# A decoder step on one core: fewer key steps carried over, unit-matrix products during the first loads, the gates' sums between tile products

## What is computed

```python
mod = silu(c) @ w_ada + b_ada                  # 3072 columns: shift, scale, gate
h = rms_norm(x, norm_g) * (1 + scale) + shift
z = h @ w_in                                   # columns split into
#   att q | k | v | silu-gate (512 each), mLSTM q,k | v | o | silu-gate, i,f gate logits, two merge gates
A = attend(q, k, v)       # 8 heads x 64; samples: top-3 past blocks of 256 keys by q . mean(k), paged cache
B = mlstm(qk, v, i, f)    # 4 heads; gates need cumsum(log sigmoid f) and a running maximum
ya = (A * silu(za)) @ w_att ; ym = (B * silu(zm)) @ w_mlstm
x = x + gate * ((sigmoid(ga) * ya + sigmoid(gm) * ym) @ w_out), then a last RMSNorm
```

## Time and profile before

| | us |
|---|---|
| median of 3 runs (lowest, highest) | 733.54 (732.51, 970.24) |
| the profiled execution, its device time | 734.37 |
| its span in the trace | 731.4 |
| busy in the span: TensorE / DVE / GpSimd / ScalarE | 685.4 / 470.9 / 429.9 / 334.2 |
| bytes moved | 144.72 MB, mean 198 GB/s |

### The profile page before, as it was taken

One profiled execution on the slowest core, in us unless ns is written; L12 is line 12 of the kernel. 1 busy time (PEld: TensorE's weight loads), 2 busy tenths in 40 slices (PEclk: granted clock), 3 DMA queues, 4 the chain that ended last, 5 costly groups with the idle time before them and its releaser, 6 DMA issues.

```text
span 731.4 us, 14741 instructions
## 1 busy us (share of the span) xinstructions
PE 685.4 (94%) x5012; PEld 611.4 (84%) x5012; DVE 470.9 (64%) x483; ACT 334.2 (46%) x726; POOL 429.9 (59%) x278
## 2 busy tenths in 40 slices
PE   1799999998989979999999999999999999999996
PEld 0477788887868858999999999997899998999974
DVE  0625579998979964995697597762445368444435
ACT  5546556656471436464464544514322224322643
POOL 4203366576756417698789688752754656566520
PEclk9997999999998999999999999999899999999999
DMA  8978359888898777387867668758475355832302
GB/s 314 340 232 252 114 159 297 245 269 266 244 268 262 243 211 214 96 242 209 242 199 209 201 199 241 219 163 226 124 199 148 99 176 155 252 96 86 87 28 90
DMA packets 156904, 144.72 MB, mean 198 GB/s; under 512 B 7547, under 2 KB 115152, under 8 KB 156852
## 3 DMA queue, kind: packets, MB, share of 16 engines
q1 hardware_dynamic: 142984, 137.15, 62.5%
q10 hardware_dynamic: 13876, 7.02, 3.2%
HBM read 135.10 MB, written 9.11 MB: 197 GB/s over the span
## 4 chain that ended last, share of the span: by engine, by line
PE 59%; SPq 12%; DVE 10%; issue 7%; POOL 5%; DMA 5%; ACT 1%; ACTq 0%; DVEq 0%; POOLq 0%
PE ps L556 42%; SPq L398 5%; SPq L399 4%; DMA sb_arenaA<-in_w_ada 3%; PE ps L990 3%; PE ps L822 2%; DVE sb_arenaA L1833 2%; POOL sb_arenaA L1563 2%; POOL sb_arenaA L1595 2%; POOL sb_wL L1517 2%; PE ps L930 1%; PE ps L590 1%; DVE sb_arenaA L1980 1%; DVE sb_arenaB L1980 1%; PE ps L783 1%
## 5 line engine op out<-in xcount | busy, mean ns | idle before, releaser
L1517 POOL TENSOR_TENSOR sb_wL<-sb_wraw,sb_wH 128x512 fp32r<-128x512 f32 (+1 forms) x168 | 222.3, 1338 | 202.0 <-ACT sb_wH L1020 183.6
L556 PE MATMUL ps<-sb_hH,sb_wH 128*128 128x260 f32 x1152 | 241.7, 292 | 0.9 <-ACT sb_arenaB L1025 0.9
L556 PE MATMUL ps<-sb_hH,sb_wL 128*128 128x260 f32 x1152 | 235.4, 286 | 0.0
L556 PE MATMUL ps<-sb_hL,sb_wH 128*128 128x260 f32 x1152 | 235.2, 286 | 0.0
L556 PEld LDWEIGHTS ps<-sb_hH,sb_wH 128*128 128x128 f32 x1152 | 181.5, 193 | 15.7 <-issue 13.4
L1020 ACT ACTIVATE sb_wH<-sb_wraw 128x512 fp32r<-128x512 f32 (+1 forms) x168 | 99.3, 612 | 195.8 <-PE ps L556 159.9
L556 PEld LDWEIGHTS ps<-sb_hL,sb_wH 128*128 128x128 f32 x1152 | 181.4, 192 | 0.0
L556 PEld LDWEIGHTS ps<-sb_hH,sb_wL 128*128 128x128 f32 x1152 | 181.0, 192 | 0.0
L1595 POOL TENSOR_TENSOR sb_arenaA<-sb_arenaA 128x2048 f32<-128x2048 f32 x28 | 101.6, 3633 | 1.7 <-DMA sb_arenaA<-in_cache_v 1.7
L1837 DVE TENSOR_REDUCE sb_arenaA<-sb_arenaA 128x2048 f32 (+1 forms) x32 | 72.9, 2284 | 3.8 <-DVE sb_arenaA L1833 2.5
L1563 POOL TENSOR_TENSOR sb_arenaA<-sb_arenaA 128x2048 f32<-128x2048 f32 x11 | 54.4, 4941 | 28.2 <-DMA sb_arenaA<-in_cache_k 28.2
(11 more groups left out here) (389 smaller groups left out, 976.6 us busy)
## 6 DMA issues: line engine op xcount, KB each, us to landing
sb_wraw<-in_w_in SPq DMA_DIRECT2D x64, 512.0 KB, 5.2
sb_arenaA<-in_cache_k SPq DMA_DIRECT2D x128, 256.0 KB, 3.1
sb_arenaA<-in_cache_v SPq DMA_DIRECT2D x128, 256.0 KB, 3.1
sb_arenaA<-in_w_ada SPq DMA_DIRECT2D x6, 2048.0 KB, 12.4
sb_arenaB<-in_state_C SPq DMA_DIRECT2D x8, 512.0 KB, 3.9
sb_wraw<-in_w_mlstm SPq DMA_DIRECT2D x8, 512.0 KB, 5.1
sb_wraw<-in_w_out SPq DMA_DIRECT2D x8, 512.0 KB, 3.8
sb_arenaB<-in_x_prompt SPq DMA_DIRECT2D x1, 2048.0 KB
```

Of the source, the lines that this page charges most:

```text
L556: last = mm(ps[:, 2 * s + a, 0:HALF], w[:, s, k, :], x[:, k, a * HALF:(a + 1) * HALF], start=(k == 0 and w is wH and x is xH), stop=(k == ...
L1517: tt(wL[:, j % 2, part], wraw[:, j % 4, part], wH[:, j % 2, part].bitcast(F32), ALU.subtract)\
```

## The change

- `keep_clock(bank, count)` multiplies the unit matrix with itself, 512 columns, into a bank that is overwritten later: seven products ahead of the first `modulation`, four ahead of the third.
- In the first pair the gates' running sums (now `forget_sums`) stand between the products of the first half of the v tile, and the two turns and the key and value transposes each move behind a further half tile; `ptrans(0)` moves ahead of the value transposes. ScalarE's `normalise(0)` and the high part of tile n + 4 move ahead of the key eviction in the first pair.
- DVE carries steps 6 and 5 into the next pair, no longer 7. In the first pair step 2 is taken ahead of head 1's maximum, and step 3 after head 1's inverse sums. In the loop the products of steps 6 and 0 are parted from their sums.
- After the last pair the fourth mLSTM tile moves ahead of the selection's products, and the sixth is multiplied whole ahead of the last `modulation`; ScalarE's high part of the sixth moves with it.

```diff
@@ -609,7 +609,12 @@
                         last = tr(ps[:, 4 + k % 4, j * P:(j + 1) * P], xt[:, j, k * P:(k + 1) * P], ident[:, :])
                     last.then_inc(t_x, 1)
 
+            def keep_clock(bank, count):
+                for _ in range(count):
+                    mm(ps[:, bank, :], ident[:, :], ident[:, :].unsqueeze(1).broadcast_to([P, TT, P]), start=True, stop=True)
+
             pe.wait_ge(consts, 2)
+            keep_clock(6, 7)
             modulation(0, 0)
             pe.wait_ge(x_nrm, 2)
             prompt_turn(range(4))
@@ -626,6 +631,7 @@
 
             pe.wait_ge(v_col, 1)
             pe.wait_ge(mod_rdy, 2)
+            keep_clock(3, 4)
             modulation(2, 2)
             ztile(0, T_ATT, hH, hL, part_ready=h_lo, parts=(0,))
             pe.wait_ge(xT_dve, 5)
@@ -680,6 +686,15 @@
                     last = mm(ps[DH * e:DH * e + DH, 7, k * P:T], vN[:, k, DH * e:DH * e + DH], pT[:, k, k * P:T],
                               start=(k == 0), stop=(k == TT - 1))
                 return last
+
+            def forget_sums(ks):
+                for j in ks:
+                    pe.wait_ge(g_dve, 3)
+                    last = mm(ps[:, 7, MH * j:MH * j + MH], upper[:, :], lf[:, j, :], start=True, stop=(j == 0))
+                    for i in range(j):
+                        last = mm(ps[:, 7, MH * j:MH * j + MH], ones[:, :], lf[:, i, :], start=False, stop=(i == j - 1))
+                    if j == TT - 1:
+                        last.then_inc(g_pe, 1)
 
             def query_copy(e, t, bank):
 
@@ -715,42 +730,41 @@
                 query_copy(0, t, 4)
                 if before:
                     pv(1).then_inc(pv_done, 1)
-                else:
-                    pe.wait_ge(g_dve, 3)
-                    for j in range(TT):
-                        last = mm(ps[:, 7, MH * j:MH * j + MH], upper[:, :], lf[:, j, :], start=True, stop=(j == 0))
-                        for i in range(j):
-                            last = mm(ps[:, 7, MH * j:MH * j + MH], ones[:, :], lf[:, i, :], start=False,
-                                      stop=(i == j - 1))
-                    last.then_inc(g_pe, 1)
                 pe.wait_ge(z_free, n + 4)
                 qk(0, t)
-                ztile(2, n + 2, hH, hL, parts=(0, 1) if before else (0,))
-                if not before:
-
+                if before:
+                    ztile(2, n + 2, hH, hL)
+                else:
+                    ztile(2, n + 2, hH, hL, parts=(0,), beside=forget_sums)
+                    ztile(2, n + 2, hH, hL, parts=(1,))
                     pe.wait_ge(g_dve, 4)
                     for j in range(TT):
                         last = tr(ps[0:MH, 7, j * P:(j + 1) * P], ec[:, j, :], ident[:, :])
                     last.then_inc(g_pe, 1)
-                    ztile(2, n + 2, hH, hL, parts=(1,))
+                    ztile(3, n + 3, hH, hL, parts=(0,))
                     pe.wait_ge(g_dve, 5)
                     for j in range(TT):
                         last = tr(ps[:, 7, MH * j:MH * j + MH], MR[:, j * P:(j + 1) * P], ident[0:MH, 0:MH])
                     last.then_inc(g_pe, 1)
-                    ztile(3, n + 3, hH, hL, parts=(0,))
+                    ztile(3, n + 3, hH, hL, parts=(1,))
                     pe.wait_ge(g_dve, 6)
                 pe.wait_ge(ya_done, t + 1)
                 for j in range(TT):
                     last = tr(ps[:, 7, j * P:(j + 1) * P], kT[:, j * P:(j + 1) * P], ident[:, :])
                 last.then_inc(kn_mm, 1)
-                ztile(3, n + 3, hH, hL, parts=(0, 1) if before else (1,))
+                if before:
+                    ztile(3, n + 3, hH, hL)
+                else:
+                    pe.wait_ge(pnorm, 2 * t + 1)
+                    ptrans(0)
                 pe.wait_ge(kn_ev, t + 1)
                 pe.wait_ge(z_free, n + 5)
                 for j in range(TT):
                     last = tr(ps[:, 7, j * P:(j + 1) * P], vT[:, j * P:(j + 1) * P], ident[:, :])
                 last.then_inc(vn_mm, 1)
-                pe.wait_ge(pnorm, 2 * t + 1)
-                ptrans(0)
+                if before:
+                    pe.wait_ge(pnorm, 2 * t + 1)
+                    ptrans(0)
                 pe.wait_ge(vn_ev, t + 1)
                 query_copy(1, t, 7)
                 qk(1, t)
@@ -849,6 +863,8 @@
             pv(1).then_inc(pv_done, 1)
             ztile(2, T_ML + 2, hH, hL)
 
+            ztile(3, T_ML + 3, hH, hL)
+
             pe.wait_ge(sel_dve, 1)
             for e in range(2):
                 last = mm(ps[:, 4, 32 * e:32 * e + 32], headsel[:, e, :], tS[:, :, :].rearrange("p a b -> p (a b)"),
@@ -858,7 +874,6 @@
                 for t in range(PAIRS):
                     last = tr(ps[0:B, 5 + a, t * P:(t + 1) * P], qkvS[:, 1 + a, t, :], ident[:, :])
             last.then_inc(sel_pe, 1)
-            ztile(3, T_ML + 3, hH, hL)
             ztile(4, T_ML + 4, hH, hL)
 
             pe.wait_ge(ya_done, 1 + PAIRS)
@@ -868,10 +883,9 @@
             last.then_inc(sel_pe, 1)
             pe.wait_ge(sel_act, 1)
             modulation(5, 6)
-            ztile(5, T_ML + 5, hH, hL, parts=(0,))
+            ztile(5, T_ML + 5, hH, hL)
             pe.wait_ge(ada_ev, 5)
             modulation(6, 6)
-            ztile(5, T_ML + 5, hH, hL, parts=(1,))
 
             pe.wait_ge(sel_dve, 3)
             mm(ps[:, 7, :], ones[0:B, :], pend.rearrange("p b n -> p (b n)"), start=True, stop=True).then_inc(sel_pe, 1)
@@ -1195,14 +1209,18 @@
                 weights(0, t)
                 samples_kept(2, n + 2, t)
                 leave(0, n + 2, vT, ACT.Copy)
+                if not before:
+                    normalise(0, t)
+                    high(0, n + 4, quad + 1)
                 act.wait_ge(kn_mm, t + 1)
                 act.wait_ge(st_k, 16 * t + 16)
                 f(kN, ps[:, 7, :].rearrange("p (j n) -> p j n", j=TT), ACT.Copy).then_inc(kn_ev, 1)
                 act.wait_ge(kn_ev, t + 1)
                 act.dma_start(rows_out(O["k_p"], t), kN).then_inc(st_k, 16)
-                normalise(0, t)
-                high(0, n + 4, quad + 1)
-                if not before:
+                if before:
+                    normalise(0, t)
+                    high(0, n + 4, quad + 1)
+                else:
                     gate_exps()
                 act.wait_ge(vn_mm, t + 1)
                 act.wait_ge(st_v, 16 * t + 16)
@@ -1231,6 +1249,7 @@
             leave(1, T_ML + 1, pre[:, 1, 3:3 + NT], ACT.Copy, chunk(preS, MH))
             high(0, T_ML + 4, T_ML // 4 + 1)
             leave(0, T_ML + 2, mvT[:, 0, :], ACT.Copy, chunk(vS, 0))
+            high(1, T_ML + 5, T_ML // 4 + 1)
             act.wait_ge(sel_pe, 2)
             for a in range(2):
                 last = f(ksN[:, a, :], ps[0:B, 5 + a, :], ACT.Copy)
@@ -1238,7 +1257,6 @@
             act.wait_ge(sel_act, 1)
             act.dma_start(O["k_s"].rearrange("o b q h d -> (o b q) (h d)"), ksN[:, 0, :]).then_inc(st_misc, 16)
             act.dma_start(O["v_s"].rearrange("o b q h d -> (o b q) (h d)"), ksN[:, 1, :]).then_inc(st_misc, 16)
-            high(1, T_ML + 5, T_ML // 4 + 1)
             leave(1, T_ML + 3, mvT[:, 1, :], ACT.Copy, chunk(vS, 1))
 
             act.wait_ge(ya_done, 1 + PAIRS)
@@ -1856,21 +1874,23 @@
                     gate_sums()
                 causal_max(0, t)
                 if before:
-                    key_step(7, t - 1)
+                    key_products(6, t - 1)
+                    inverse_sums(0, t)
+                    key_sums(6, t - 1)
+                    key_step(5, t - 1)
+                    key_products(0, t)
+                    causal_max(1, t)
+                    key_sums(0, t)
                 else:
                     gate_max()
-                inverse_sums(0, t)
-                if before:
-                    key_step(6, t - 1)
-                    key_step(5, t - 1)
-                else:
+                    inverse_sums(0, t)
                     gate_stabilisers()
                     states_convolved()
-                key_step(0 if before else 1, t)
-                causal_max(1, t)
-                key_step(3, t)
+                    key_step(1, t)
+                    key_step(2, t)
+                    causal_max(1, t)
                 inverse_sums(1, t)
-                for s in (1, 2, 4) if before else (2, 4):
+                for s in (3, 1, 2, 4, 7) if before else (3, 4, 7):
                     key_step(s, t)
                 output_gated(t)
 
@@ -1904,7 +1924,7 @@
             dve.wait_ge(ya_done, 1 + PAIRS)
             dve.wait_ge(z_free, T_ATT + 4 * PAIRS + 1)
             tt(tS[:, :, :], qkvS[:, 0], qkvS[:, 1], ALU.mult).then_inc(sel_dve, 1)
-            for s in (7, 6, 5):
+            for s in (6, 5):
                 key_step(s, LAST)
             for slot in range(KV_SLOTS):
                 dve.wait_ge(page_free[slot], 1 + 2 * PAIRS)
```

## The result

The changed kernel takes 737.56 us (median of 20 runs, 733.24 to 744.07) against 732.57 us for the kernel before in the same measurement: ratio 1.0103, 95% interval 1.0076 to 1.013. The ratios here are worked out from the fast executions alone and need not equal the quotient of the medians, which is 1.0068 in this case; differences of a few tenths of a per cent should be read with that in mind. The prediction of 737.0 us, some 0.5% above before, was right in time and range; it is inside what was called "same". Whether its steps were right is the question of what follows.

The account below looks back on a forecast made before the run. SP's page-load issues were taken to pace the attention stage, its end tied to slot 3's first release. +6.0 - 2.6 = +3.4 on the profiled 734.37, less 0.8 to the median, gave 737.0 us, range 729.5 to 741.0.

Parts of the forecast that it names:

- Part 1: Unit-matrix products at the start: third modulation block shorter, -1.2 us for all of TensorE up to 60 us.
- Part 2: First pair, gates' sums between tile products: TensorE's gain of over 4 us is gone once ScalarE starts its exponentials.
- G = 67.9: First pair: the time in us at which the gates' sums end on TensorE.
- Part 3: First pair, DVE and GpSimd excluding each other: slot 3 free at 100.4 us against 94.37, +6.0 us.
- rival A: First pair: GpSimd and DVE collide, +6.0 or milder +3.8 us, giving 737.0 or 734.8 us; chance 0.60.
- B: First pair: DVE's step 1 product starts before GpSimd's first low part, slot 3 free at 93.5, 730.1 us; chance 0.17.
- D: First pair: TensorE stays at half clock to about 73 us, 4 us later plus the collision, 741 us; chance 0.10.
- the collision: First pair: DVE's step 1 product is held up by GpSimd's step 3 product, about 9 us by the rule, not 2.3.
- SP's +6.0 passes whole to 248.5: Attention stage: the later release of slot 3 delays SP's page loads and the stage's end by the full 6.0 us.
- Rival C: Attention stage paced by DVE's tail or transfers, not SP; the late slot doesn't pass on, 730.9 us; chance 0.13.
- Part 4: Pairs 1 to 3, two key steps carried instead of three: 0 us, bounds -2.3 and +2.3.
- Part 5: Turn into the second branch: half tile fills TensorE's hole ahead of the last modulation block, L877 earlier, -2.6 us.

Follow-up runs that it names:

- first experiment: Changed kernel with DVE's first-pair order of before: step 2 behind head 1's maximum, step 3's sum ahead of head 1's inverse sums; 732.19 us, ratio 1.0023.
- old carry in changed: Changed kernel with step 7 carried into the next pair again and DVE's loop as before, the first pair's new order kept; 738.62 us, ratio 1.0119.
- slot 3 early in before: Kernel before, first pair: GpSimd's step 3 product ahead of its low part, DVE's sum behind head 0's inverse sums; 731.26 us, ratio 1.0009.
- The carry alone: Kernel before with only DVE's loop and carry changed, step 7 summed in its own pair; 732.6 us, ratio 1.0035.
- all of DVE as before: Changed kernel with DVE's first pair and loop both as in the kernel before; 730.16 us, ratio 1.0002.
- the last experiment: Changed kernel with slot 3 released early and step 2 back behind head 1's mask, maximum and inverse sums; 729.47 us, ratio 0.9971.

## Why the prediction came out right

**Part 1, -1.2 us.** Right at its place: third block 1.92 us, fourth block at 38.24 instead of 39.37. The seven first products took 9.19 us and end at 16.8, in the range given, and cost at most the 1.1 us by which the first block starts later (16.75 against 15.68). That the gain arrives at the end was not shown; the run without the products is not slower. Nor do the traces show that the products made the third block short: of the five other kernels without them, three have it at 1.92 us too (2.77 and 2.86 in the others). Over all fourteen traces the fourth block starts at 38.3 us on average with the products and at 39.0 without, so 0.7 us is what the record supports, not 1.2.

**Part 2, G = 67.9.** Measured 67.98, and the maximum of head 0 at 71.1 as worked out. The clock held from 60 to 80 us (granted 1.00). Missed: it fell in the next stretch instead, at the scores of head 1, 2.2 us longer. This was harmless only because DVE was busy with the steps 1 and 2 and its mask had to wait anyway. (The "20 tiny products" are 20 records, ten products in the code.)

**Part 3, +6.0.** Event by event nearly exact: low part 76.23 (76.3 predicted), GpSimd's product ahead of DVE's, step 1's product up to 85.38 (85.7), mask 92.61 (92.7), slot 3 free at 99.99 (100.4), SP at 100.8. So rival A, not B (DVE's product first) and not D. The page of the Trainium skill, SBUF — State Buffer, section SBUF: two separate sides, is borne out for the whole instruction (6.50 us for 2.29). What was incomplete is the cause that rival A names, "the collision". With DVE's old order behind it the same collision costs nothing that can be seen (1.0008, and 1.0023 with the new carry). By the rows it takes both: the collision lengthens step 1's product by 4.2 us, and step 2, some 5 us, stands ahead of the mask. Without step 2 there the mask comes at 88.3 (first experiment). Without the collision it would come near 88.4 (an estimate, 92.6 - 4.2; in the run with ScalarE's old order, where the collision is absent, DVE was ready for it at 87.4). Either alone is covered by the wait for head 1's scores, 5.16 us before; together they are not. The sum of step 3 behind the inverse sums adds its part to the slot (99.99 against 94.37). How the loss divides among these was not shown, since no run removes the collision and leaves the rest as it is.

**"SP's +6.0 passes whole to 248.5".** The size was right, +6.8 at the last key sum. The reason was half right. A slot at 100 us does reach DVE as a late page (old carry in changed), and in the changed kernel as a late step 7, for which DVE waits 8.13 us ahead of the gating. But the stage was not "tied to the moment at which slot 3 is first freed": freed 16 us earlier it brings nothing (slot 3 early in before), and with a free slot the place of step 2 still moves the last key sum by 7.1 us (252.3 against 245.2). The prediction used the late mask of head 1 only as a step on the way to slot 3 and never priced its own way to the gating over ScalarE's normalising and TensorE's turn, although the 3.00 us that DVE waited for the value products (L680) ahead of the gating were to be had from the trace of before. In the changed kernel TensorE idles 4.01 us for the normalising on this way. Rival C was wrong in effect: the delay did arrive; its premise, that SP's idle time is no bottleneck, was right of the kernel before.

**Part 4, 0 (bounds -2.3 and +2.3).** Not refuted and not confirmed. The carry alone measures 1.0035 [1.0, 1.007], anything from 0 to 5 us, and its last key sum is 2.5 us later, of which 1.3 come from before the carry acts. The two kernels that differ in the carry alone, DVE's order of before and all of DVE as before, end it at 248.0 and 248.7 us, and the old carry in the changed kernel changes nothing that can be seen (255.1 against 255.3). The number of operations is the same, as said; what the prediction left out is that step 7's sum now waits for GpSimd in each pair, against which the waits for pages shrink.

**Part 5, -2.6.** 2.5 us between the last issue of w_ada and L891. That it reaches the end of the program was not shown (0.9999 [0.9964, 1.0034] for it alone).

**Sum.** The change forecast was +6.0 - 2.6 = +3.4 us; the 0.8 only leads from the profiled execution to the median. In the traces the sum holds term by term, +6.8 - 2.5 = +4.3 at L891 and +3.8 at 520 us. The times say more: the medians differ by 5.0 us, and the ratio of 1.0103 is +7.5 us, with an interval from 5.6 to 9.5. So the terms that were priced explain about half of what the ratio shows, and that 737.0 met 737.56 so closely is in part luck: the kernel before had 733.54 in the prediction and 732.57 beside the changed kernel. Where the other 3 us arise stays open. The clock is a candidate: the mean granted clock of the changed kernel's 20 executions was 0.969, that of the kernel before in the four groups 0.973 to 0.975, and among the executions of the kernel before 0.001 less goes with some 0.4 to 0.5 us more (correlation -0.7 to -0.8), which would make some 2 to 3 us, an estimate. No run tested it.

## What to carry over

A long wait of a queue is the bottleneck only if what it loads is waited for at its landing. DVE waited 6.3 us for pages in the whole kernel before, and 5.5 us between 95 and 250 us even with the slot free 16 us earlier; 18.1 us of idle SP said nothing, and with the slot freed early SP waited 18.4 us all the same, for the next ones. Ahead of a chain that runs over three engines (mask, exponentials, normalising, turn, value products), an operation of 4.6 us that "only fills" costs its whole length as soon as the chain's input is there first: put filling work behind the chain's step, and take it ahead only where the trace shows idle time that long. If two engines lock each other out, look for the idle time of the one that can go early: GpSimd's product of step 3 fitted into the 10.66 us ahead of its low part, and the collision was gone. And a delay from one engine and a delay from one's own order can each be free and cost only together: price them in one sum, against the idle time that covers them.

## What the runs showed of the hardware

A small DVE operation can pay for a large one of GpSimd: 128x16 took 4.43 us where 0.18 is usual (in the kernel before with slot 3 early, at 66.47 us, GpSimd's product from 66.36 on). It goes the other way as well, in GpSimd's timeline of the same run, where DVE's product of 2.82 us (99.18) overlaps:

```profile
66.36 4.52 POOL L1563 TENSOR_TENSOR sb_arenaA<-sb_arenaA 128x2048 f32<-128x2048 f32 x1
...
99.81 6.63 POOL L1563 TENSOR_TENSOR sb_arenaA<-sb_arenaA 128x2048 f32<-128x2048 f32 x1
```

I had not expected the clock to move about so much. A half-clock stretch that an edit removes can turn up elsewhere (63 to 74 us before, 82 to 89 and 98 to 106 in the changed kernel; in the last experiment, slot 3 early and mask before step 2, none of these places has one), and where the others fall differs from execution to execution. Equal programs spread over 724 to 738 us, which is more than any part of this change. The row of the granted clock does not show everything either: before, it reads 1.00 from 14 to 20 us, yet the first block of w_ada at 15.68 took 3.56 us, as long as at half clock, where the same work takes 1.92.
